# Prompt attention with its probabilities transposed in 32-by-32 blocks on VectorE and its value product in 32-row tiles

## What is computed

```
k_nope = einsum('bsc,chd->bshd', c_kv, w_a_uk)
v      = einsum('bsc,chd->bshd', c_kv, w_a_uv)
# per block of 128 queries
sc = (einsum('bqhd,bkhd->bhqk', qn_b, k_nope) + einsum('bqhd,bkd->bhqk', qr_b, k_r)) * ATTN_SCALE
sc = where(k_pos <= q_pos, sc, -inf)
p  = softmax(sc, axis=-1)
o  = einsum('bhqk,bkhd->bqhd', p, v)
```

## Time and profile before

| what | value |
|---|---|
| time, median of 3 runs | 1532.52 us (1532.19 to 1536.1) |
| the profiled execution | 1532.18 us, its span 1530.5 us |
| PE busy | 1505.8 us, 98% |
| DVE busy | 934.7 us, 61% |
| ACT busy | 551.6 us, 36% |
| POOL busy | 243.8 us, 16% |
| moved by DMA | 117.73 MB |

### The profile page before, as it was taken

The page is one execution under the profiler, slowest core; times in us unless marked ns, Lnnn a source line. Parts: engine busy times, 40 slices in busy tenths (PEclk is TensorE's granted clock), DMA queues, the critical chain, the costliest instruction groups (busy, mean ns, idle before and its releaser), DMA issues.

```text
span 1530.5 us, 32080 instructions
## 1 busy us (share of the span) xinstructions
PE 1505.8 (98%) x11757; PEld 1372.2 (90%) x11757; DVE 934.7 (61%) x1722; ACT 551.6 (36%) x1187; POOL 243.8 (16%) x431
## 2 busy tenths in 40 slices
PE   8999999999999999999999999999999999999998
PEld 7988888888887677778899999999999999999996
DVE  5675667666667788367664645554544545554557
ACT  5465665556664223232331312212131312112146
POOL 2010011101115541000030211212020311112000
PEclk9999999999999999999999999999999999999999
DMA  7112121111133998351220202022020202021003
GB/s 231 51 40 56 38 41 30 39 38 37 23 105 93 301 309 274 112 169 42 81 86 28 69 14 69 15 67 68 20 62 27 69 14 69 14 69 55 1 28 125
DMA packets 158655, 117.73 MB, mean 77 GB/s; under 512 B 55263, under 2 KB 145821, under 8 KB 158416
## 3 DMA queue, kind: packets, MB, share of 16 engines
q1 hardware_dynamic: 143280, 94.40, 20.9%
q10 hardware_dynamic: 11664, 11.44, 2.3%
q0 software_dynamic: 3600, 10.43, 2.1%
HBM read 106.08 MB, written 14.34 MB: 79 GB/s over the span
## 4 chain that ended last, share of the span: by engine, by line
PE 49%; DVE 1%; issue 0%; ACT 0%; DVEq 0%
PE banks L2120 16%; PE banks L2121 16%; PE banks L2122 16%; PE banks L2203 0%; PE banks L2205 0%; PE banks L2204 0%; PE banks L2190 0%; DVEq L1939 0%; DVE weight_stage L2523 0%; DVE down_stage L2523 0%; DVE weight_stage L2536 0%; DVE down_stage L2536 0%; DVE f_stats L2495 0%; ACT up_hi L2345 0%; ACT up_hi L2341 0%
## 5 line engine op out<-in xcount | busy, mean ns | idle before, releaser
L2120 PE MATMUL banks<-act_hi,up_hi 128*128 128x352 f32 (+2 forms) x1040 | 335.5, 323 | 0.8 <-PEq L1691 0.8
L2122 PE MATMUL banks<-act_hi,up_lo 128*128 128x352 f32 (+2 forms) x1040 | 335.4, 323 | 0.0
L2121 PE MATMUL banks<-act_lo,up_hi 128*128 128x352 f32 (+2 forms) x1040 | 335.1, 322 | 0.0
L2120 PEld LDWEIGHTS banks<-act_hi,up_hi 128*128 128x128 f32 x1040 | 195.3, 188 | 1.0 <-issue 1.0
L2121 PEld LDWEIGHTS banks<-act_lo,up_hi 128*128 128x128 f32 x1040 | 195.5, 188 | 0.0
L2122 PEld LDWEIGHTS banks<-act_hi,up_lo 128*128 128x128 f32 x1040 | 195.4, 188 | 0.0
L2423 DVE TENSOR_TENSOR o_t<-o_t,banks 128x352 f32<-128x352 f32 x240 | 121.0, 520 | 95.1 <-PE banks L2122 94.9
L2402 DVE SCALAR_TENSOR_TENSOR conv_out<-conv_in,conv_now,conv_out 128x1072 f32<-128x1072 f32 x42 | 64.7, 1540 | 185.2 <-ACT conv_out L2276 185.2
L1118 DVE TENSOR_REDUCE neg_max<-banks 128x1 f32<-128x896 f32 (+7 forms) x128 | 96.6, 755 | 105.5 <-PE banks L880 104.6
L2267 ACT ACTIVATE conv_in<-banks 128x352 f32<-128x352 f32 x84 | 36.4, 459 | 336.4 <-PE banks L2122 336.4
L2120 PE MATMUL banks<-gated_hi,down_hi 128*128 128x352 f32 x480 | 155.9, 325 | 0.0
(11 more groups left out here) (342 smaller groups left out, 3066.7 us busy)
## 6 DMA issues: line engine op xcount, KB each, us to landing
weight_stage<-in_w_f_up SPq DMA_DIRECT2D x44, 512.0 KB, 4.6
page_slot<-in_cache_kv_latent SPq DMA_DIRECT2D x100, 128.0 KB, 3.7
down_stage<-in_w_f_down SPq DMA_DIRECT2D x22, 512.0 KB, 4.3
page_slot<-in_cache_kv_latent ACTq DMA_DIRECT2D x51, 128.0 KB, 3.8
rope_rows<-in_cache_k_rope SPq DMA_DIRECT2D x256, 16.0 KB, 2.0
rope_slot<-rope_rows SPq DMA_DIRECT2D x16, 256.0 KB, 4.1
z<-in_x_prompt SPq DMA_DIRECT2D x8, 512.0 KB, 3.4
o_blocks<-o_t POOLq DMA_DIRECT2D x30, 128.0 KB, 2.2
```

The source lines that it names most:

```text
L2120: nc.tensor.matmul(o, ws[0], xs[0], start=first, stop=False)
L2121: nc.tensor.matmul(o, ws[0], xs[1], start=False, stop=False)
L2122: return nc.tensor.matmul(o, ws[1], xs[0], start=False, stop=last)
```

## The change

**Units.** A pair still has 16 units, now one head behind the other, tiles in the order 7, 0, 6, 1, 5, 2, 4, 3.

**Probabilities.** DVE transposes them itself, from SBUF to SBUF, each 32x32 block on its own (`probs_t`). In such a layout a block of 32 keys lies in each 32-row quarter of the partitions: quarter i holds 32 of a tile's 128 queries for all keys. So the value product contracts over 32 rows: for each of up to 32 blocks of 32 keys, for two sides c (four query tiles each, `SIDES`) and four quarters i, one matmul of 32x64 weights, whose columns are the 32 queries of quarter i of all tiles of the side that reach this block: 128, 96, 64 or 32. The eight (c, i) are eight tiles of the array, with banks 4 to 7 as outputs. A head has 240 such matmuls, 480 records.

**V.** The product needs each block of 32 keys in all four quarters. DVE transposes V's projection from PSUM in 32x32 blocks (`v_t`), SP stores it to DRAM (`v_rows`, 4 DMAs per pair, runs of 128 bytes) and loads it back four times, once per quarter (4 DMAs per head). The PE transposes t0 and t1 and ACT's copies go.

**Reciprocals.** Once per head, one reciprocal reads the eight row sums of a query row, each repeated 64 times, and writes 512 columns (`inverse`); four PE transposes turn it.

**Others.** The low halves of q (but for the first pair) and of the next pair's weights move from DVE to POOL (`q_low`, `split_first`, `split_second`). The stores of o move from POOL's queue to SP's. K's halves of the second head are taken after the last scores of the pair before. The first cached pages (`sp_pages` and `pool_pages` of 0) are loaded behind the seventh pair and no longer in the first; their place holds V. The last head's value product comes after the first cached scores, as the last group's did.

The core of the diff:

```diff
-UNITS = [(g, hh, r) for g in (3, 2, 1, 0) for hh in range(2) for r in range(2)]
-NEXT_AT = {4: "wt", 5: "v0", 6: "v1", 8: "k1", 9: "q02", 10: "q12", 11: "q01", 12: "q11", 14: "k0", 15: "q00", 16: "q10"}
-INV_AT = {7: 3, 10: 2, 13: 1}
-VALUES_AT = {5: (3, 0, 2), 7: (3, 2, 4), 9: (2, 0, 2), 11: (2, 2, 4), 14: (1, 0, 4)}
+UNITS = [(hh, t) for hh in range(2) for t in (7, 0, 6, 1, 5, 2, 4, 3)]
+OWN_AT = {0: ["q12", "q11"], 3: ["ql"], 4: ["q10"]}
+NEXT_AT = {5: ["wt"], 6: ["q02"], 7: ["q01"], 8: ["q00"], 11: ["k1"], 12: ["k0"], 13: ["v0"], 14: ["v1"]}
+INV_AT = {1: 1, 9: 0}
+VALUES_AT = {2: 1, 10: 0}
+OUT_AT = {3: 1, 11: 0}
+SIDES = [(0, 2, 5, 7), (6, 4, 3, 1)]
...
+            def values(p, hh):
+                pe.wait_ge(xt_ok, p * NU + 8 * hh + 8)
+                pe.wait_ge(v_in[hh], (WD_IN if hh == 0 else 0) + 64 * (p + 1))
+                if hh == 0:
+                    if p + 1 < PAIRS:
+                        taken(p + 1, "q01")
+                        taken(p + 1, "q00")
+                        taken(p + 1, "wt")
...
+                for j in range(4 * TT - 4):
+                    for c in range(2):
+                        if slots_at(c, j) is None:
+                            continue
+                        a, b = slots_at(c, j)
+                        blocks = slice(block_of(c, a, j), block_of(c, b - 1, j) + 1, STRIDE[c])
+                        for i in range(4):
+                            r = slice(32 * i, 32 * i + 32)
+                            last = nc.tensor.matmul(ps[64 * c:64 * c + 64, 4 + i, 32 * a:32 * b], v[r, j, :], x[r, hh, blocks, :],
+                                                    start=j == 0, stop=j == last_block(c))
...
+            def probs_t(p, n):
...
+                nc.vector.transpose(out, prob[n % 2][:, 0:wd]).then_inc(xt_ok, 1)
+            def inverse(p, hh):
+                dve.wait_ge(pr, p * NU + 8 * hh + 8)
+                if head(p, hh) > 1:
+                    dve.wait_ge(fin, head(p, hh) - 1)
+                nc.vector.reciprocal(rb[:, :, :], sums[:, hh, :, :].rearrange("p s (c o) -> p (s c) o", o=1)
+                                     .to_broadcast([P, 8, V_HEAD])).then_inc(rv_ok, 1)
...
             for p in range(PAIRS):
                 more = p + 1 < PAIRS
                 for n in range(NU + 1):
+                    if n in (8, NU):
+                        inverse(p, n // 8 - 1)
+                    if n:
+                        probs_t(p, n - 1)
+                    if n in OUT_AT and (p or n > 3):
+                        o_done(p - OUT_AT[n], OUT_AT[n])
                     if n + 1 < NU:
                         row_max(p, n + 1)
+                    if n == NU and more:
+                        row_max(p + 1, 0)
+                        k_low(p + 1, "k1", 1)
+                        k_low(p + 1, "k0", 1)
+                    for q, name in units(p, n - 1):
+                        if name[0] == "v":
+                            v_t(q, name)
+                        elif name[0] == "q" and name != "ql":
+                            q_scale(q, name)
...
+            def store_v(p):
+                sp.wait_ge(pj_dve, dve_count(p, "v1"))
+                for a in range(4):
+                    sp.dma_start(m.v_rows[p % 2, a // 2, :, :, 32 * (a % 2):32 * (a % 2) + 32],
+                                 vq[32 * a:32 * a + 32, :, :].rearrange("k a (j d) -> k (a j) d", d=32)).then_inc(v_out, 16)
```

More of the change, by code:

```diff
@@ new lines, in load_v, with gather @@
+            def load_v(p, hh):
+                for i in range(4):
+                    sp.dma_start(v_blocks(p, hh)[32 * i:32 * i + 32, :], m.v_rows[p % 2, hh].rearrange("k j d -> k (j d)")).then_inc(v_in[hh], 16)
+            def gather(first, end):
+                for at in range(4 * first, min(4 * end, DEC_BATCH * N_PAGES), 4):
+                    f, b = at // 8, at % 8 // 4
+                    pages = nc.values_load_multi_w_load_instructions(m.pages[0:1, at:at + 4], [sp.engine])[1]
+                    for j, page in enumerate(pages):
+                        sp.dma_start(m.rope_rows[f // 2, :, f % 2, b, j, :],
+                                     io["cache_k_rope"][bass.ds(page, 1)].rearrange("o p c -> (o p) c")).then_inc(gathered, 16)
@@ new lines, in _ @@
+            sp.wait_ge(d_const, 64)
+            sp.wait_ge(w.hi_ok, 1)
+            sp.wait_ge(w.lo_ok, w.lo_count(0, "k"))
+            sp.wait_ge(pj, pj_count(0, "wt"))
+            w.load(sp, io, 1)
+            store_v(0)
+            gather(0, 1)
+            v_stored(sp, 0)
+            load_v(0, 0)
+            load_v(0, 1)
+            for p in range(PAIRS - 1):
+                if p:
+                    sp.wait_ge(pv, head(p - 1, 1))
+                    load_v(p, 1)
+                    store_o(p - 1, 1)
+                gather(10 * p + 1, 10 * p + 4)
+                if p + 2 < PAIRS:
+                    sp.wait_ge(w.lo_ok, w.lo_count(p + 1, "q1"))
+                    sp.wait_ge(pj, pj_count(p + 1, "wt"))
+                    w.load(sp, io, p + 2)
+                gather(10 * p + 4, 10 * p + 8)
+                store_o(p, 0)
+                gather(10 * p + 8, 10 * p + 11)
+                store_v(p + 1)
+                v_stored(sp, p + 1)
+                if p + 2 < PAIRS:
+                    load_v(p + 1, 0)
@@ L792, in _ @@
             queries(nc, m, 0)
-            for g in (3, 2):
-                store_o(PAIRS - 1, g)
+            pool.wait_ge(pv, head(PAIRS - 1, 0))
+            pool_pages(nc, io, m, pool, 5)
         @block.tensor
@@ new lines, in inverse_rows @@
+            def inverse_rows(p, hh):
+                bank = INV_BANK
+                pe.wait_ge(rv_ok, head(p, hh))
+                if hh == 0 and p + 1 < PAIRS:
+                    taken(p + 1, "q02")
+                elif hh == 0:
+                    pe.wait_ge(iv_ok, head(p - 1, 1))
+                elif p + 1 < PAIRS:
+                    pe.wait_ge(iv_ok, head(p, 0))
+                else:
+                    bank = 4
+                    pe.wait_ge(of_ok, head(p, 0))
+                for slot in range(4):
+                    last = nc.tensor.transpose(ps[:, bank, slot * P:(slot + 1) * P],
+                                               rb[:, 2 * slot:2 * slot + 2, :].rearrange("p c d -> p (c d)"), m.ident[:, :])
@@ L1143, in o_done @@
[L1143 to L1152 removed]
+                if n % 8 == 0 and p:
+                    dve.wait_ge(pv, head(p - 1, hh))
@@ L1220 @@
 NEW_BANK = 3
-NEW_AT = {10: 0, 11: 1, 12: 2, 13: 3}
-FIRST_KEYS_AT = {3 + i: (i // 5, KEY_PARTS[i % 5]) for i in range(10)}
+NEW_AT = {11: 0, 12: 1, 13: 2, 14: 3}
+FIRST_KEYS_AT = {5 + i: (i // 5, KEY_PARTS[i % 5]) for i in range(10)}
 def page_load(nc, io, m, eng, f, some, landed):
@@ L1451, in _ @@
             k = 0
+            for i in range(2):
+                pool.wait_ge(m.o_st[i], 32 * PAIRS)
             for q in range(1, DPAIRS):
```

612 lines of the change are left out of this document (283 added, 329 removed).

## The result

| | before | after |
|---|---|---|
| median of 4 runs | 1533.5 us | 1714.7 us |
| lowest to highest | 1532.2 to 1536.1 | 1712.6 to 1714.9 |
| time after over time before | | 1.1176, 95% interval 1.1156 to 1.1195 |
| span of the profiled execution | 1530.5 us | 1713.0 us |
| mean granted TensorE clock | 1.00 | 0.94 |

The change makes the kernel 181 us slower. I had said 1551 us, 19 us slower, and a range that ends at 1580: the sign was right and the size was wrong by a factor of ten.

The account below looks back on a forecast made before the run. TensorE alone was taken to set attention's pace; a pair went from 49.2 to 51.4 us. Seven periods gave +15.4, pair 1 -1, the end +4.5: +19 on 1532.5, so 1551 us, range 1508 to 1580.

Parts of the forecast that it names:

- With 0.3 for entering and leaving the tiled mode 5.3: New value product on TensorE: 5.0 us of rounds plus 0.3 for the mode, 5.3 us a head, +10.6 a pair.
- rival (4): Value product: narrow matmuls bound by issue, 13.6 us a head, +8.3 x 16 = +133, kernel 1684 us; chance 0.05.
- eight records have started within 0.06 us: Decode's cached scores, earlier trace: ground for 5.3 us a head, not 13.6 at 0.028 us a record.
- rival (5): Value product: rounds of 64 and 32 columns not below 0.1 us, 6.7 a head, +22, 1573 us; chance 0.09.
- 51.4: Forecast time of a head pair in attention: 42.7 + 3.7 + 3.0 + 2.0 us, against 49.2 before.
- 8.7 a pair forecast: TensorE's waits in a pair of attention: 3.7, 3.0 at a pair's end and 2.0 in mid-pair.
- The third scores of a pair: At a pair's end, TensorE waits 3.0 us here behind VectorE's reciprocal, transpose and maximum and ScalarE's exp.
- 3.7 us forecast between ends of 0.7 and 8.3: The 512-wide reciprocal on VectorE, once per head, taken at 7 ns an element: 3.7 us each.
- one us moves seven pairs by 11.7 and the last by about 2: Reciprocal's price in attention: 3.0 us less saves 5.0 of wait a pair; one us moves 13.5 together.
- I had +4.5: Last pair and its end: +2.5 for VectorE's work, +2 for cached scores behind a reciprocal and the whole last product.
- the ring's waits: Attention's cycle of scores, maximum, exp, scores, with two places: a unit's scores need the exp of the unit two before.
- My chance of 0.30 for faster: Whole kernel: chance given to a result faster than before, against 0.60 for slower and 0.10 for same.

Follow-up runs that it names:

- the fine version: Changed kernel with the reciprocal of 8 sums copied 64 wide and the value product dealt out in 32 to 48 records between other matmuls: 1675.8 us.
- the narrow reciprocal: Changed kernel with the reciprocal taken of a row's 8 sums, then copied 64 wide, instead of taken 512 wide: 1695.8 us.

## Why the prediction was wrong

**The value product: the step that failed.** "With 0.3 for entering and leaving the tiled mode 5.3" a head; it was 12.4 and 13.4, +15.2 us a pair, 106 over seven periods and a good part of the rest behind them. Three parts are in it.

The first are the rests, 9.6 of the 15.2. That is the mechanism of rival (4), which I gave 0.05: its price was 0.028 us a record, the whole of the earlier trace rows, and I set it aside for "eight records have started within 0.06 us". Those eight were instructions already at hand. The earlier trace rows by itself could not have told more: 144 records in 4.07 us, 18 rounds at 0.226, is both "256 columns at the array's pace" and "as fast as 128 records come". Other rows can. In the trace of before the packets of the instruction queue around this row start 6 us apart, none between 541.5 and 546 us, and in the kernel after the same 144 records take 6.5 us at a granted clock of 0.60. So the earlier trace rows was the array's pace, and that its 0.028 us is also that of a piece, some 3.6 us for 128 records, is a coincidence: rival (4) had the mechanism without a row for it and its price by luck. What I never asked is how fast instructions come when 128 records run in 1.7 us and not in 3.6. The 25 ns between starts that the Trainium skill states (TensorE: Matmul & The Clock Gate, "Wait — 56ns, not 53.3ns?"), which gave 1658, are not what acts here: 48 records take 0.69 us, 14 ns each, in the fine version.

The second part is the array's pace, 1.8 us a head. Without its rests (5.4 us) the first head's product takes 7.1 us, where I had 5.3 (some 0.5 of the 1.8 are its last 39 records, at the half level of the clock): a stretch of 128 records, 16 rounds, takes 1.73 us from 96 columns on and 1.60 from 64 on, at the full clock 0.108 and 0.100 us a round where I had 0.085 and 0.057. That is rival (5), 6.7 a head, which I held at 0.09. The third part is the clock inside the second head's product, at 0.67: without its rests (4.3 us) it takes 9.1 us, 2.0 more than the first.

Rival (4)'s pair would be 68.0 us, 51.4 and twice 8.3. The measured 69.9 has 1.4 less of product, 4.6 of low clock elsewhere and 1.3 less of waits, which is 13 of the 31 us between its 1684 and the measured 1714.7. The other 17 or so stand from the last pair on.

**The clock: missing altogether.** I priced waits at their own length. After them, and after the product's rests, TensorE runs stretches at 1.2 GHz: per pair 69.9 - 25.8 of product - 7.4 of other waits (44.1 / 6 over the same six pairs) leaves 36.7, where I had 32.1 of work. The 4.6 are the low clock outside the product. Without the product it is 5.3.

**Waits: right.** 8.7 a pair forecast, 7.4 here, 9.5 without the product. The third scores of a pair, for which I had 3.0 us, stood 2.36, each head's product 1.19 and 1.39 (I had 1.2 and 0.8, for the scaled q; what ended last was the transpose of probabilities right behind it on VectorE):

```profile
303.21 0.51 PE L914 MATMUL banks<-k_hi,q_hi 128*128 128x512 f32 x1 [2.36 <-ACT probs L1088]
...
307.01 2.03 PE L1026 MATMUL banks<-probs_t,o_t 32*64 32x128 f32 x122 [1.39 <-DVE probs_t L1224]
```

The pair by steps: 51.4 + 15.2 (product) + 4.6 (clock) - 1.3 (waits) = 69.9.

**The reciprocal: right.** 3.7 us forecast between ends of 0.7 and 8.3, 3.3 measured, 6.5 ns an element:

```profile
L1231 DVE RECIPROCAL inv_rows<-sums 128x512 f32<-128x512 f32 x16 | 53.2, 3324 | 0.0
...
L1224 DVE STREAM_TRANSPOSE probs_t<-probs 128x1024 f32<-128x1024 f32 x16 | 19.7, 1230 | 0.2
L1189 DVE STREAM_TRANSPOSE o_t<-banks 128x512 f32<-128x512 f32 x16 | 11.0, 689 | 0.0
```

My choice within wide ends came out well, but no row stood between 3 and 16 ns an element to support it: luck in part. The 4.5 us that I had drawn from the Trainium skill's repeat count of 8 (VectorE: DVE Perf Modes, "First, the fixed hardware budget") is above the row. The transposes on VectorE cost what the earlier trace rows said.

Its worth, "one us moves seven pairs by 11.7 and the last by about 2", agrees in the number and not in the mechanism. 2.4 us less gave 30 us without the product, for which this rate gives 32. But the waits fell by 2.9 us a pair, where the rate asks for 4.1, and the clock, which the rate doesn't have, gave the rest. With the product 2.4 us less gave only 19, since the rests grew as the waits fell.

**GpSimd, SyncE, V through memory: right for the kernel of the change.** TensorE waited 0.4 us a pair for GpSimd's low halves. SyncE's queue was harmless at 47.7 us a pair and more, and showed up only at 42. V's rows too were waited for only then, but with the narrow reciprocal their loads seem to hold up the instructions of the product. None of these parts was undone by itself.

**The last pair and the end.** I had +4.5. The last K transposes to decode took 38.7 us more, the rest 17.2. Before decode stand three products and a stretch at a clock of 0.64, behind it one more. Decode's first cached scores are the same 144 records as in the earlier trace rows; right behind a wait of 4.7 us, at a granted clock of 0.60, they take 6.5 us to the next kind instead of 4.07:

```profile
650.17 1.08 PE L1044 MATMUL banks<-ident,inv_rows 128*128 128x128 f32 x4 [4.69 <-issue]
651.18 6.68 PE L1414 MATMUL banks<-o_t,q_blocks 32*64 32x256 f32 x144
657.69 2.81 PE L1026 MATMUL banks<-probs_t 32*64 32x128 f32 x190
```

**Could the idea pay at all?** Off TensorE go 17.1 us a pair (7.9, 0.7, 8.5). The product without any rest is 7 to 8 us a head, 14 to 16 a pair. So even with instructions always at hand and the clock full, 1 to 3 us a pair are to be had, before the ring's waits, which were 7.4. My chance of 0.30 for faster rested on 10.6 for the two products.

## What to carry to other kernels

Count instructions before columns: here 128 matmul records with their weight loads make one 16 KB piece, and each piece costs TensorE some 3.5 us or more; work on narrow tiles that runs through a piece faster is paid at that price, and splitting it takes the rests away only if every 128 records in a row last that long. A row priced by the column says nothing of a supply that is counted in instructions: the earlier trace rows needed a piece every 6 us, the new product one in under 2. Ask that of every much denser stretch, and price the supply as a case with a real chance. And a wait that is new to a TensorE that was always busy costs more than its length, since here it came with work at half the clock.

## What the runs showed of the hardware that I had not expected

- Rests every 128 matmul records, 1.0 to 2.5 us each, with a 16 KB instruction packet beginning only once TensorE has entered the piece before: 3.5 to 4 us from piece to piece, at 32 columns as at 128 and at half the clock as at the full one; 6.1 us (164.10 to 170.18) where the DMA engines were busy with V's rows. Longer matmuls took a rest away only inside a piece, by making it last: the 176 records from 262.64 on run through behind ten longer ones of the same piece.
- With waits of 0.5 to 2.4 us, 9.5 us in a pair of 47.7, a clock of 0.89 is granted where 1.00 was before; at 6.6 us of waits in a pair of 42.2 (26.2 in four pairs, 119 to 288 us) 0.95.
- A reciprocal of 128x512 takes 3324 ns, the copy that widens 8 values to 512 takes 696.
- Eight narrow matmul records start within 0.06 us, but a run of 48 takes 14 to 18 ns each, with 64 to 96 columns, and a run of 128 12.5 to 13.5.
